# First products of a stage from high parts alone, first high parts made by ScalarE from PSUM, and fewer filler products, in a two-block transformer kernel

## The reference

```python
def modulate(x, gain, shift, scale):
    return rms_norm(x, gain) * (1 + scale[:, None, :]) + shift[:, None, :]
...
        h = modulate(x, norm_mix[i], sh_m, sc_m)
        j = i // N_MIXERS
        if i % N_MIXERS == 0:
            y = moba_attention(h, w_qkv[j], w_o[j], q_gain[j], k_gain[j])
        else:
            y = short_conv(h, w_in[j], conv_w[j], w_out[j])
        x = x + g_m[:, None, :] * y
        h = modulate(x, norm_ffn[i], sh_f, sc_f)
        x = x + g_f[:, None, :] * swiglu(h, w_gate_up[i], w_down[i])
```

## Time and profile before

| | before |
|---|---|
| median of 3 runs | 1356.95 us |
| the profiled execution | 1358.56 us, of which 1356.5 us are its span |
| TensorE busy | 1306.8 us (96%) |
| VectorE, ScalarE busy | 1013.1 us (75%), 752.5 us (55%) |
| mean granted TensorE clock | 0.992 |

### The profile page before, as it was taken

How to read it: one execution, slowest core, us unless ns; L and a number is a source line. 1 busy time by engine, 2 the same in 40 slices (tenths; PEclk the granted TensorE clock), 3 DMA queues, 4 the chain that set the end, 5 groups by cost and what they waited for, 6 DMA issues and landing times.

```text
span 1356.5 us, 19325 instructions
## 1 busy us (share of the span) xinstructions
PE 1306.8 (96%) x7400; PEld 1114.5 (82%) x7400; DVE 1013.1 (75%) x1104; ACT 752.5 (55%) x775; POOL 80.2 (6%) x83
## 2 busy tenths in 40 slices
PE   5999999999999999999999999999989989999995
PEld 3988878888899878888999978888879968888884
DVE  2788878888877774544675768899986466899997
ACT  2665533333544544433474457877766575677773
POOL 0100000000000000000000010000011200000020
PEclk9999999999999999999999999999999999999998
DMA  9987489998585476557443343999995622599991
GB/s 377 388 316 247 164 283 308 307 307 304 200 296 186 133 271 203 180 184 244 162 145 125 119 146 127 316 346 343 351 376 188 189 63 93 193 322 344 345 344 63
DMA packets 201612, 325.60 MB, mean 240 GB/s; under 512 B 9328, under 2 KB 142128, under 8 KB 200000
## 3 DMA queue, kind: packets, MB, share of 16 engines
q1 hardware_dynamic: 187952, 272.52, 59.3%
q0 software_dynamic: 13584, 52.03, 11.4%
HBM read 321.36 MB, written 3.15 MB: 239 GB/s over the span
## 4 chain that ended last, share of the span: by engine, by line
PE 86%; DVE 7%; ACT 3%; DMA 3%; issue 1%; SPq 0%; DVEq 0%; ACTq 0%
PE ps L2462 24%; PE ps L2464 24%; PE ps L2463 24%; DVE w_low L1506 2%; ACT w_high L739 2%; PE ps L3001 2%; PE ps L3245 1%; DMA scratch<-in_w_ada 1%; DMA raw<-in_w_mem_kv 1%; PE ps L2835 1%; PE ps L3140 1%; PE ps L2574 1%; DVE h_low L2331 1%; DMA ones<-in_k_ones 1%; PE ps L2562 1%
## 5 line engine op out<-in xcount | busy, mean ns | idle before, releaser
L1506 DVE TENSOR_TENSOR w_low<-raw,w_high 128x2048 fp32r<-128x2048 f32 (+1 forms) x248 | 580.1, 2344 | 227.8 <-ACT w_high L739 225.7
L739 ACT ACTIVATE w_high<-raw 128x2048 fp32r<-128x2048 f32 (+1 forms) x248 | 472.8, 1907 | 281.9 <-PE ps L2464 260.3
L2462 PE MATMUL ps<-w_high,h_high 128*128 128x512 f32 (+1 forms) x872 | 343.5, 394 | 6.1 <-DVE h_low L1647 2.3
L2464 PE MATMUL ps<-w_high,h_low 128*128 128x512 f32 (+1 forms) x872 | 336.7, 386 | 0.0
L2463 PE MATMUL ps<-w_low,h_high 128*128 128x512 f32 (+1 forms) x872 | 336.3, 386 | 0.0
L2462 PEld LDWEIGHTS ps<-w_high,h_high 128*128 128x128 f32 x872 | 163.9, 188 | 39.7 <-issue 4.5
L2464 PEld LDWEIGHTS ps<-w_high,h_low 128*128 128x128 f32 x872 | 163.8, 188 | 33.7
L2463 PEld LDWEIGHTS ps<-w_low,h_high 128*128 128x128 f32 x872 | 164.1, 188 | 30.8 <-issue 0.2
L2462 PE MATMUL ps<-h_high,w_high 128*128 128x256 f32 x592 | 171.3, 289 | 0.9 <-DVE h_low L1647 0.9
L2464 PE MATMUL ps<-h_high,w_low 128*128 128x256 f32 x592 | 167.5, 283 | 0.0
L2463 PE MATMUL ps<-h_low,w_high 128*128 128x256 f32 x592 | 167.4, 283 | 0.0
(11 more groups left out here) (424 smaller groups left out, 1405.4 us busy)
## 6 DMA issues: line engine op xcount, KB each, us to landing
raw<-in_w_down SPq DMA_DIRECT2D x120, 512.0 KB, 4.9
raw<-in_w_gate_up SPq DMA_DIRECT2D x88, 512.0 KB, 5.5
scratch<-in_w_ada POOLq DMA_DIRECT2D x40, 1024.0 KB, 5.6
raw<-in_w_gate SPq DMA_DIRECT2D x76, 512.0 KB, 5.1
raw<-in_w_up SPq DMA_DIRECT2D x76, 512.0 KB, 6.3
raw<-in_w_qkv SPq DMA_DIRECT2D x24, 512.0 KB, 16.5
raw<-in_w_o SPq DMA_DIRECT2D x24, 512.0 KB, 4.7
raw<-in_w_in SPq DMA_DIRECT2D x24, 512.0 KB, 5.4
```

The lines of the kernel that those rows point to most:

```text
L739: act.activation(wh[u % SPL][:, :, 0:w], raw[u % RAW][:, :, 0:w], ACT.Copy).then_inc(h_split, 1)
L1506: dve.tensor_tensor(wl[u % SPL][:, :, 0:w], raw[u % RAW][:, :, 0:w], wh[u % SPL][:, :, 0:w].bitcast(F32), ALU.subtract).then_inc(l_split, 1)
L2462: pe.matmul(o, h1, h2, start=start, stop=False, skip_group_check=True)
L2464: return pe.matmul(o, l1, h2, start=False, stop=stop, skip_group_check=True)
```

## The change

In a stage's first unit the matmuls are reordered (`fresh_products`, `first_outs`): first, for each of two groups, `w_high` and `w_low` by `h_high`, behind a wait for `hh_ready` (the high parts); then, group by group, `w_high` by `h_low`, behind `h_ready`. The second unit keeps the old order. `transposed_mod` makes the high parts of groups 0 and 1 on ScalarE straight from PSUM, with scale and shift in the instruction; VectorE's copies of them in `small` remain, group 1 ahead of group 0, since the low parts are still taken from them. The transposes come in the order 0, 1, 2, 3. The filler products go from 10 to 4 (qkv), 4 to 2 and 6 to 3 (feed-forwards), 6 to 3 (convolution). The number of other matmuls is the same.

```diff
@@ ScalarE, transposed_mod
                 def first_high(g):
 
-                    act.wait_ge(v_ready, v.up())
-                    act.activation(hh[:, 2 * g:2 * g + 2, :], shifted_parts(g), ACT.Copy).then_inc(hh_ready, 1)
+                    if g:
+                        act.wait_ge(v_ready, v.up())
+                        v.up()
+                    else:
+                        act.wait_ge(xt_ready, xt.value(1))
+                    for q in range(2):
+                        k = 2 * g + q
+                        i = act.activation(hh[:, k, :], ps[:, 4 + g, q * S:(q + 1) * S], ACT.Identity, bias=shift[:, k:k + 1],
+                                           scale=scale[:, k:k + 1])
+                    i.then_inc(hh_ready, 1)
                     hhr.up()
...
-                shifted(2)
                 first_high(0)
                 first_high(1)
+                shifted(2)
                 high(2)
                 shifted(3)
                 high(3)
@@ VectorE, transposed_mod
-                for g in range(2):
-                    dve.wait_ge(xt_ready, xt.up())
-                    xt.up()
+                for g in (1, 0):
+                    if g:
+                        dve.wait_ge(xt_ready, xt.value(2))
+                    else:
+                        dve.wait_ge(hh_ready, hhr.value(1))
                     for q in range(2):
...
@@ TensorE
+            def fresh_products(outs, rows, operands):
+
+                for g in range(2):
+                    pe.wait_ge(hh_ready, hr.value(g + 1) + others[0])
+                    for b, o in enumerate(outs):
+                        for k in (2 * g, 2 * g + 1):
+                            w_h, w_l, h_h, h_l = operands(b, k)
+                            pe.matmul(o, *((h_h, w_h) if rows else (w_h, h_h)), start=k == 0 and (rows or b % 2 == 0), stop=False, skip_group_check=True)
+                            pe.matmul(o, *((h_h, w_l) if rows else (w_l, h_h)), start=False, stop=False, skip_group_check=True)
+                for g in range(2):
+                    pe.wait_ge(h_ready, hr.up())
+                    for b, o in enumerate(outs):
+                        for k in (2 * g, 2 * g + 1):
+                            w_h, w_l, h_h, h_l = operands(b, k)
+                            i = pe.matmul(o, *((h_l, w_h) if rows else (w_h, h_l)), start=False, stop=False, skip_group_check=True)
+                i.then_inc(unit_used, 1)
+                used.up()
...
@@ chunk, the first two units of a stage with features as outputs
-                        unit_features(n[0], pair, w // P, UK * q, q == 0, q == 1, fresh).then_inc(unit_used, 1)
-                        used.up()
+                        if fresh and q == 0:
...
+                            fresh_products([ps[:, pair + b // 2, (b % 2) * S:(b % 2 + 1) * S] for b in range(w // P)], False,
...
@@ the feed-forward's gate_up and out_rows have the same branch (fresh_products, first_outs)
...
-            def transposes(src, order=(0, 2, 1, 3)):
+            def transposes(src, order=range(4)):
...
-            keep_busy(10, 0)
+            keep_busy(4, 0)
             pe.wait_ge(mod_taken, mtk.up())
...
-            keep_busy(4, 0)
+            keep_busy(2, 0)
...
-            keep_busy(6, 0)
+            keep_busy(3, 0)
```

More of the change, by code:

```diff
@@ L818, in shifted @@
                 def shifted(g):
-                    xt.up(2)
-                    act.wait_ge(xt_ready, xt.value())
+                    act.wait_ge(xt_ready, xt.value(g + 1))
                     for q in range(2):
@@ L844, in transposed_mod @@
                 high(3)
+                xt.up(4)
             def transposed():
@@ L2498, in unit_features @@
                 return i
+            others = [0]
+            def fresh_products(outs, rows, operands):
[14 more added lines that the diff above has]
+                used.up()
             evac, r0r = Count(lin_evac), Count(row0_ready)
@@ L2512, in chunk @@
                         pe.wait_ge(l_split, lsp.up())
-                        unit_features(n[0], pair, w // P, UK * q, q == 0, q == 1, fresh).then_inc(unit_used, 1)
-                        used.up()
+                        if fresh and q == 0:
+                            u = n[0] % SPL
+                            fresh_products([ps[:, pair + b // 2, (b % 2) * S:(b % 2 + 1) * S] for b in range(w // P)], False,
+                                           lambda b, k: (wh[u][:, k, b * P:(b + 1) * P], wl[u][:, k, b * P:(b + 1) * P], hh[:, k, :], hl[:, k, :]))
+                        else:
+                            unit_features(n[0], pair, w // P, UK * q, q == 0, q == 1, fresh).then_inc(unit_used, 1)
+                            used.up()
                     n[0] += 1
@@ L2521, in _, with first_outs @@
             olr = Count(ol_ready)
+            def first_outs():
+                pe.wait_ge(l_split, lsp.up())
+                u = n[0] % SPL
+                for g in range(2):
+                    pe.wait_ge(hh_ready, hr.value() + g + 2)
+                    for t in range(TT):
+                        for k in (2 * g, 2 * g + 1):
+                            tok = slice(t * P, (t + 1) * P)
+                            pe.matmul(ps[:, 4 + 2 * t, :], hh[:, k, tok], wh[u][:, k, :], start=k == 0, stop=False, skip_group_check=True)
+                            pe.matmul(ps[:, 4 + 2 * t, :], hh[:, k, tok], wl[u][:, k, :], start=False, stop=False, skip_group_check=True)
+                for g in range(2):
+                    pe.wait_ge(ol_ready, olr.up())
+                    for t in range(TT):
+                        for k in (2 * g, 2 * g + 1):
+                            tok = slice(t * P, (t + 1) * P)
+                            i = pe.matmul(ps[:, 4 + 2 * t, :], hl[:, k, tok], wh[u][:, k, :], start=False, stop=False, skip_group_check=True)
+                i.then_inc(unit_used, 1)
+                used.up()
             def out_rows(fresh=False, begun=False):
@@ L2526, in out_rows @@
                     for q in range(1 if begun and c == 0 else 0, 2):
+                        if fresh and c == q == 0:
+                            first_outs()
+                            n[0] += 1
+                            continue
                         unit_rows(n[0], lambda t: ps[:, 4 + 2 * t + c, :], UK * q, NC, q == 0, q == 1, c == q == 1,
@@ L2545, in turn_halves @@
                     pe.wait_ge(xn_ready, xn.up())
-                    for g in (0, 2, 1, 3):
+                    for g in range(4):
                         for k in range(2):
@@ L2820, in gate_up @@
                         u = n[0] + j + q
+                        if fresh and q == 0:
+                            fresh_products([ps[:, t, :] for t in range(TT)], True,
+                                           lambda t, k: (wh[u % SPL][:, k, :], wl[u % SPL][:, k, :],
+                                                         hh[:, k, t * P:(t + 1) * P], hl[:, k, t * P:(t + 1) * P]))
+                            continue
                         for t in range(TT):
@@ L3040, in _ @@
             out_rows(fresh=True)
+            others[0] = 4
             sc0 = Count(scaled0)
```

## The result

| | before | after |
|---|---|---|
| median (20 runs each, in turns) | 1357.66 us | 1361.08 us |
| lowest, highest | 1355.09, 1361.34 | 1356.71, 1367.79 |
| profiled execution: span, mean granted clock | 1356.5 us, 0.992 | 1363.7 us, 0.990 |

The ratio is 1.0032, 95% interval 1.0023 to 1.0041: slower, where I had forecast a loss of 2.1 us that couldn't be told from none. The executions after the change lie in two heaps, 12 of 20 up to 1362.3 us and 8 from 1364.5; the profiled one is of the upper. By themselves the twelve have a median of 1359.56 us, 1.9 above the kernel before and near my 1359.1; the eight have 1365.8. Among the experiments' executions two lie far off (2188 us in straight_only, 4697 us in old_tail), and one of the kernel before (1870 us); medians and ratios leave them out.

What follows compares the result with a forecast made beforehand. TensorE, busy 96% of 1356.5 us, was taken as the bound. A loss of 0.7 us at the convolution plus 1.4 for the clock made 2.1: 1359.1 us from 1356.95, range 1354.6 to 1362.4.

Steps and rivals of the forecast that it cites:

- Starts: First units start 1.7 us earlier at the convolution and both feed-forwards, 2.4 us earlier at qkv.
- ScalarE's tail: ScalarE's last copy of `h` ends 0.67, say 0.7 us later (0.5 at qkv), moving the next `w_high` and `w_low`.
- Convolution: Second unit 0.7 us later, after a gap of some 2.35 us; the clock falls, costing 1.4 us more.
- Rival A: The gap at the convolution leaves the clock up, only 0.7 us is lost: 1357.7 us; chance 0.27.
- Feed-forwards: Second units start about as before, after gaps of some 1.5 us, without a fall of the clock.
- rival B: The clock also falls at the feed-forwards, losing 1.5 us at each: 1362.1 us, slower; chance 0.20.
- qkv at 0: At qkv the second unit starts at 44.9 against 44.89; the 2.4 us won come back, with a 1.3 us gap.
- Output product at 0: Up to 1.5 us can be won, but the norm's chain behind it doesn't move: 0 taken.
- The sum: 0.7 us lost at the convolution and 1.4 for the clock: 2.1 us, median 1359.1, not told from no change.
- Rival C: Second units aren't late, starts are kept: 1354.9 us with no longer tail, 1348 with weights in time; chance 0.16.

Runs made afterwards that it cites:

- straight_only: The kernel before with only the new `transposed_mod` and order of transposes: 1358.92 us, ratio 1.0012 to the kernel before.
- old_tail: The changed kernel with `transposed_mod` and the order of transposes as in the kernel before: 1355.27 us, ratio 0.9997 to the kernel before.
- outs_only: The kernel before with only the output product's new order (`first_outs`), stage entries and filler as before: 1356.4 us, ratio 1.0001.
- conv_fill: The changed kernel with 11 constant products between first and second unit at the convolution: 1360.6 us, ratio 1.0031 to the kernel before.
- filler_back: The changed kernel with the old counts of constant products (10, 4, 6 and 6): 1359.94 us, ratio 1.0023 to the kernel before.
- second_early: The changed kernel with the second unit's weights split before or amid the preparation of `h` at four stages: 1352.58 us, ratio 0.9967.
- after_gain: The changed kernel, VectorE adding two quarters of the rows before waiting for transfers in the norm behind the output product: 1358.35 us, ratio 1.0016.
- second_gain: second_early with the edit of after_gain: 1351.69 us, ratio 0.9962 to the kernel before.
- best: second_gain with qkv's extra splits behind ScalarE's first two high parts and VectorE's first two low parts: 1350.87 us, ratio 0.9961.
- norm_fill: The changed kernel with constant products where TensorE waits for the norm behind each output product: 1365.61 us, ratio 1.0061.
- second_outs: second_early with the output product in the old order: 1352.58 us, ratio 0.9967 to the kernel before.

## Why the prediction was wrong in its verdict, and where it held

**Starts: right, but for qkv.** Against the same stage of outs_only the first units start 1.6 us sooner at all four entries (at the convolution at 358.24, of which 0.63 was lost ahead of it, against 359.19). I had 1.7 at three, and 2.4 at qkv.

**ScalarE's tail: right.** I had 0.67 to 0.7 us. Counted from the first transpose of the stage (355.02 in outs_only, 355.72 after), ScalarE's next `w_high` starts 5.85 us later in the old form and 6.59 in the new: 0.74. First outs_only, then after:

```profile
355.02 1.91 PE L2573 MATMUL ps<-ident,rows 128*128 128x128 f32 x16
...
360.38 0.60 ACT L836 ACTIVATE h_high<-ps 128x512 fp32r<-128x512 f32 x1
360.87 1.90 ACT L739 ACTIVATE w_high<-raw 128x2048 fp32r<-128x2048 f32 x1
```

```profile
355.72 1.91 PE L2609 MATMUL ps<-ident,rows 128*128 128x128 f32 x16
...
357.07 1.02 ACT L835 ACTIVATE h_high<-ps,mod_shift,mod_scale 128x256 fp32r<-128x256 f32 x2 [2.22 <-PE ps L2609]
...
361.81 0.60 ACT L843 ACTIVATE h_high<-ps 128x512 fp32r<-128x512 f32 x1
362.31 1.90 ACT L739 ACTIVATE w_high<-raw 128x2048 fp32r<-128x2048 f32 x1
```

The pair of straight high parts takes 1.02; I took 0.99.

**Convolution: right.** A gap of 2.35 us was forecast and 2.38 measured. 0.7 for the weights and 1.4 for the clock were forecast; straight_only and conv_fill give 0.75 and 0.78 without the clock, after less conv_fill gives 1.5 for it. Rival A (the clock stays up there) is out.

**Feed-forwards: right but for 0.12 and 0.15.** Gaps of 1.43 and 1.41 us, where 1.5 was forecast, and the clock at 1.00: rival B is out.

**qkv at 0: wrong.** This step took its start from an execution that itself ran at half clock until about 39 us, and so got a gap of 1.3 us between the units. Undisturbed, the first unit starts at 35.36 and not 36.65, the gap is 2.11, the second unit is 0.5 us later than in outs_only, and in three of five profiles the clock fell, for about 1.5 us more. Nor does the filler cover the wait for `h_low` there, as I had it: in outs_only TensorE waits 1.08 us for it. I should have asked what the entry looks like when that disturbance is away.

**Output product at 0: wrong in size.** "The change moves none of this chain" did not hold for its first link: I took the row transfer's 7.3 us as fixed. It is not, and when it is late, a gap of 1.41 us comes ahead of the one of 1.32, and the stretch took 6.2 us more in the profiled execution. I had even forecast a longer wait of the transposes, as time that was won before and given back; that such a wait could cost the clock I weighed at the entries only. About how often, by the times and mean clocks alone: 8 of 20 executions after the change lie in an upper heap, two of 12 in conv_fill, at most one of 10 in filler_back, three of 11 in old_tail, one of 5 in second_early and none of 11 in outs_only, which all have this norm and the new order. None of the 23 with the sums put first lies so far off (after_gain, second_gain, best); the highest of after_gain, 1362.79 at a mean clock of 0.991, comes nearest.

**The sum.** By the table the entries lose 3.05 us in an execution like the profiled one up to 705 us, against a forecast of 2.1, before any fall of the clock at qkv; the median moved by 3.4. The median hides two heaps: the lower one moved by 1.9, close to the forecast, and the upper one, by its profile, is the norm. That 1.9 comes out so near 2.1 is in part luck, since the executions of before carry a disturbance at qkv that the forecast did not know of, and how many do no run here shows. The time lay in my range, and the chance for "slower" was 0.28.

**Rival C named the cause.** "If the tail were no longer than before" is old_tail: 0.65 and 0.63 us won at the feed-forwards, where C had 0.8 and 0.75. "If weights were made in time besides" is second_early: 1.26 to 1.73 at three entries, where C had 1.7. At qkv C failed: it had 0.5 and 2.4, and measured were a loss of 0.26 in old_tail, where the clock fell to 0.50 behind a wait of 1.45 us, a gain of 0.43 in second_early and none in best. What costs at the entries is the straight high parts as a longer ScalarE queue ahead of the next weights; TensorE's order of passes, with the fewer constant products, was worth about 1 us up to 705 us on its own (old_tail: -0.97 there), which the medians can't tell from nothing.

**Open.** What makes the last row transfer land after 7.2 to 9.1 us. That weight loads issued nearer to it delay it is not borne out: the next ones are issued 0.5 us behind it in outs_only, filler_back and norm_fill, where it took 7.2 to 7.4, as well as after the change and in second_early, where it took 9.0; and in second_outs they come 1.45 us behind it, and it took 9.1. Open too is why the same gap of 2.11 us takes the clock in some executions and not in others, and one of 1.3 to 1.4 us at the norm in second_gain and not in outs_only.

## What to carry to other kernels

An earlier start is worth only what the next operand's arrival allows: follow the queue of the engine that does the new work to its next customer, and price the lateness there. Follow it to the end of the stage, too: a start that is kept can come back as a wait further on, as at qkv in best. Splitting the second unit's weights first turned the same change from a loss of 0.3% into a gain of 0.3%. Time that is won at a start and given back in one wait isn't neutral, since TensorE's clock can go with it: at the convolution that was 1.5 of the 2.3 us lost. And an execution that is itself disturbed at a place is no base for a price at that place.

## What the hardware showed that I had not expected

The length of a gap did not tell what the clock did. At the norm, two gaps of 1.41 and 1.32 us with 1.1 us of transposes between them were followed by some ten us at half clock, about three times as long as behind the single gap of 2.38 us at conv. At the same place two gaps of 1.05 and 1.32 us in old_tail and a single one of 1.32 in outs_only left the clock at 1.00, and a single one of 1.37 in second_gain was followed by 3.4 us at half clock. And one 64 KB transfer of the same place took from 7.2 to 9.1 us from issue to landing in kernels that move the same bytes.
